# Summing both squared tiles of a pair on TensorE in the second and third pre-norm of a layer

## The reference, cut to what matters

```
def rmsnorm(x, g):
    xf = x.astype(F32)
    y = xf * lax.rsqrt(jnp.mean(xf * xf, axis=-1, keepdims=True) + RMS_EPS)
    return (y * g.astype(F32)).astype(x.dtype)
...
    h = rmsnorm(x, g[0]) * (1 + m[:, :, 0, 1]) + m[:, :, 0, 0]
    x = x + 0.5 * m[:, :, 0, 2] * rmsnorm(swiglu(h, wg[0], wu[0], wd[0]), g[1])
    h = rmsnorm(x, g[2]) * (1 + m[:, :, 1, 1]) + m[:, :, 1, 0]
    p = h @ w_in
...
    x = x + m[:, :, 1, 2] * rmsnorm(y, g[3])
    h = rmsnorm(x, g[4]) * (1 + m[:, :, 2, 1]) + m[:, :, 2, 0]
    x = x + 0.5 * m[:, :, 2, 2] * rmsnorm(swiglu(h, wg[1], wu[1], wd[1]), g[5])
```

## Time and profile before

| | |
|---|---|
| median of 3 runs | 1708.38 us (1708.3 to 1711.51) |
| span of the profiled execution | 1706.8 us (no other time is given for it) |
| PE, matmul | 1607.5 us busy, 94% of the span |
| VectorE (DVE) | 899.6 us busy, 53% |
| ScalarE (ACT) | 765.5 us busy, 45% |
| chain that ended last | PE 87%, DVE 6%, issue 3%, DMA 2%, ACT 2% |
| mean granted TensorE clock | 0.985 of full speed |

### The profile page before, as it was taken

How to read it: one execution, slowest core, us unless ns; L and a number is a source line. 1 busy time by engine, 2 the same in 40 slices (tenths; PEclk the granted TensorE clock), 3 DMA queues, 4 the chain that set the end, 5 groups by cost and what they waited for, 6 DMA issues and landing times.

```text
span 1706.8 us, 26956 instructions
## 1 busy us (share of the span) xinstructions
PE 1607.5 (94%) x9434; PEld 1462.8 (86%) x9434; DVE 899.6 (53%) x1597; ACT 765.5 (45%) x1176; POOL 17.8 (1%) x39
## 2 busy tenths in 40 slices
PE   6799999998988899999989999999898889999996
PEld 2399989996966699989979998999696669998996
DVE  5655544336685655544336554533667565554433
ACT  2355544325535555543255544432552555554332
POOL 0000000000000000000000000000000000000000
PEclk9999999999999999999999999999999999999998
DMA  6833685345501433474343368534550144337331
GB/s 232 333 107 125 249 294 182 130 159 182 181 1 38 173 123 123 137 282 138 129 167 100 124 247 293 191 124 165 181 181 1 36 163 130 124 126 298 132 124 65
DMA packets 70613, 268.20 MB, mean 157 GB/s; under 512 B 9387, under 2 KB 10444, under 8 KB 69900
## 3 DMA queue, kind: packets, MB, share of 16 engines
q1 hardware_dynamic: 67164, 248.96, 41.7%
q0 software_dynamic: 3376, 18.35, 2.8%
HBM read 260.73 MB, written 6.55 MB: 157 GB/s over the span
## 4 chain that ended last, share of the span: by engine, by line
PE 87%; DVE 6%; issue 3%; DMA 2%; ACT 2%; POOL 0%; DVEq 0%; SPq 0%; ACTq 0%; POOLq 0%
PE bank L529 26%; PE bank L531 25%; PE bank L530 25%; PE bank L538 4%; PE bank L867 1%; PE bank L829 1%; DVE y L1271 1%; DMA w_m<-w_mod 1%; DVE rstd L1266 1%; PE bank L753 1%; PE bank L617 1%; DMA f_cst<-tneg 1%; DVE sb_s L1457 1%; ACT prob_t L1068 1%; PE bank L856 1%
## 5 line engine op out<-in xcount | busy, mean ns | idle before, releaser
L1207 DVE TENSOR_TENSOR w_lo<-w_raw,w_hi 128x1024 fp32r<-128x1024 f32 (+2 forms) x288 | 373.6, 1297 | 527.5 <-ACT w_hi L927 526.6
L529 PE MATMUL bank<-h_hi,w_hi 128*128 128x386 f32 (+1 forms) x1760 | 606.3, 344 | 1.3 <-DVE w_lo L1207 0.8
L531 PE MATMUL bank<-h_hi,w_lo 128*128 128x386 f32 (+1 forms) x1760 | 596.1, 339 | 0.0
L530 PE MATMUL bank<-h_lo,w_hi 128*128 128x386 f32 (+1 forms) x1760 | 595.5, 338 | 0.0
L927 ACT ACTIVATE w_hi<-w_raw 128x1024 fp32r<-128x1024 f32 (+2 forms) x288 | 322.1, 1118 | 528.2 <-PE bank L531 527.6
L529 PEld LDWEIGHTS bank<-h_hi,w_hi 128*128 128x128 f32 x1760 | 332.0, 189 | 20.9 <-issue 14.0
L530 PEld LDWEIGHTS bank<-h_lo,w_hi 128*128 128x128 f32 x1760 | 332.8, 189 | 1.2
L531 PEld LDWEIGHTS bank<-h_hi,w_lo 128*128 128x128 f32 x1760 | 332.3, 189 | 0.0
L530 PE MATMUL bank<-hid_lo,w_hi 128*128 128x384 f32 x704 | 238.4, 339 | 0.0
L529 PE MATMUL bank<-hid_hi,w_hi 128*128 128x384 f32 x704 | 238.4, 339 | 0.0
L531 PE MATMUL bank<-hid_hi,w_lo 128*128 128x384 f32 x704 | 238.4, 339 | 0.0
(11 more groups left out here) (194 smaller groups left out, 1123.5 us busy)
## 6 DMA issues: line engine op xcount, KB each, us to landing
w_raw<-w_gu SPq DMA_DIRECT2D x176, 512.0 KB, 3.3
w_m<-w_mod SPq DMA_DIRECT2D x160, 512.0 KB, 6.3
w_raw<-w_dn SPq DMA_DIRECT2D x64, 704.0 KB, 4.0
w_raw<-w_in SPq DMA_DIRECT2D x26, 512.0 KB, 3.4
w_raw<-w_out SPq DMA_DIRECT2D x16, 512.0 KB, 3.4
cst<-consts POOLq DMA_DIRECT2D x8, 688.0 KB, 5.9
spec<-f_spec POOLq DMA_DIRECT2D x2, 2304.0 KB, 8.2
spc<-spec POOLq DMA_DIRECT2D x8, 576.0 KB, 5.1
```

Of the source, the lines that this page charges most:

```text
L529: mm(out, w_hi[:, wn, c], rhs_hi, start=first, stop=False)
L530: mm(out, w_hi[:, wn, c], rhs_lo, start=False, stop=False)
L531: return mm(out, w_lo[s][:, c], rhs_hi, start=False, stop=last)
L1207: TT(w_lo[unit % RAW][:, 0:n], w_raw[unit % RAW][:, 0:n], w_hi[:, unit % HIS, 0:n], ALU.subtract).then_inc(unit_lo.sem, 1)
```

## The change

VectorE's add of the two squared tiles goes, in the second and third pre-norm of each layer. PE waits for ScalarE's squares themselves and multiplies both squared tiles of a pair with the matrix of ones, two matmuls in place of one, all accumulated in the same bank; this is the code that the first pre-norm already used. ScalarE now waits for PE's reading of a buffer (xsq_used) before it squares into it again. The semaphore xsq_added goes.

```diff
                 for c in range(4):
-                    if n:
-                        pe.wait_ge(xsq_added.sem, xsq_added.at(layer, 4 * n + c - 3))
-                        last = mm(bank[STAT][:, 0:T], ones[:, :], sq[:, c % 2, :], start=c == 0, stop=c == 3)
-                    else:
-
-                        pe.wait_ge(xsq_done.sem, xsq_done.at(layer, c + 1))
-                        for k in range(2):
-                            last = mm(bank[STAT][:, 0:T], ones[:, :], xsq[:, c % 2, k, :], start=c == 0 and k == 0,
-                                      stop=c == 3 and k == 1)
+                    pe.wait_ge(xsq_done.sem, xsq_done.at(layer, 4 * n + c + 1))
+                    for k in range(2):
+                        last = mm(bank[STAT][:, 0:T], ones[:, :], xsq[:, c % 2, k, :], start=c == 0 and k == 0,
+                                  stop=c == 3 and k == 1)
                     last.then_inc(xsq_used.sem, 1)
...
-                    if n:
-                        act.wait_ge(xsq_added.sem, xsq_added.at(layer, 4 * n + c - 5))
-                    else:
-                        act.wait_ge(xsq_used.sem, xsq_used.at(layer, c - 1))
+                    act.wait_ge(xsq_used.sem, xsq_used.at(layer, 4 * n + c - 1))
                     A(xsq[:, c % 2, :, :], x[:, 2 * c:2 * c + 2, :], ACT.Square).then_inc(xsq_done.sem, 1)
...
-            dve.sem_inc(xsq_added.sem, 2)
...
-                if n:
-                    dve.wait_ge(xsq_done.sem, xsq_done.at(layer, 4 * n + c + 1))
-
-                    dve.wait_ge(xsq_used.sem, xsq_used.at(layer, 4 * n + c - 1))
-                    TT(sq[:, c % 2, :], xsq[:, c % 2, 0, :], xsq[:, c % 2, 1, :], ALU.add).then_inc(xsq_added.sem, 1)
                 for k in (2 * c, 2 * c + 1):
```

More of the change, by code:

```diff
@@ L339, in build @@
         x_new = S("x_new", 3 * 4, 4)
-        xsq_done, xsq_added, xsq_used = S("xsq_done", 12), S("xsq_added", 8, 2), S("xsq_used", 12, 2)
+        xsq_done, xsq_used = S("xsq_done", 12), S("xsq_used", 12, 2)
         pre_sd = S("pre_sd", 3)
```

## The result

The changed kernel takes 1714.93 us (median of 7 runs, 1713.57 to 1716.24) against 1708.38: 1.0037 of the time before, 95% interval 1.0026 to 1.0047, or 4.4 to 8.0 us more. It is slower by about 6.3 us where 4.3 were forecast, within the range given. The profiled execution took 1713.57 us itself, with a span of 1712.0 us, 5.2 us more than the profiled span of before.

The account below looks back on a forecast made before the run. The prediction took PE, busy in 94% of the span, to bound the kernel. Added matmuls 10.4 less earlier start 4.9 less waits 1.2 made +4.3 us onto 1708.38: 1712.7 us, range 1709.6 to 1716.4.

Parts of the forecast that it names:

- PE's added work: Four more statistics matmuls of 384 columns at each of four places, 16 times 0.65 us: 10.4 us lost.
- The earlier start: PE's first statistics matmul hangs on ScalarE's first square, not the add: 1.37 or 1.09 us a place, 4.9 us gained.
- The new wait: ScalarE's third and fourth squares wait for PE's reading of the buffer: costed at nothing, without cover up to 1.4 us a place.
- three signs of being wrong: PE waiting for the fourth square or a remainder; the clock at 1.00 through a place; places ending no later than before.
- the step on TensorE's clock: Low-clock stretches after PE's first statistics matmul, 3.1 to 5.6 us, stay as long, counted from the new start: no cost.
- The waits that go: PE's waits for VectorE between first and fourth statistics matmul, 0.11, 0.22, 0.59 and 0.27 us, vanish: 1.2 us gained.
- Rival 1: The clock rises at the same instants as before despite PE's earlier start: 2.5 us more lost, +6.8, 1715.2 us; chance 0.16.
- the forecast's assumption: At each place the low-clock stretch lasts as long as before, counted from PE's new start, costing nothing more.
- Rival 2: The clock rises early, after 3.1 us at each place: +2.4, 1710.8 us; chance 0.11.
- Rival 3: PE starts before the clock falls at all places, so low stretches go: -3.7, 1704.7 us, faster; chance 0.07.
- Rival 4: All the added work lands, as work starting earlier ends in another wait: +10.4, 1718.8 us; chance 0.04.

Follow-up runs that it names:

- the halves: The change in the second pre-norm of each layer alone, and in the third alone: 1709.89 and 1711.27 us against 1708.72 for the kernel before.
- rounded squares: Changed kernel with squares and ones in the rounded float type: 1704.23 us in all three pre-norms; 1702.89, later 1702.21, in second and third alone.
- the first pair: Kernel before with the change for the first pair of the second and third pre-norm alone, VectorE adding the other three: 1708.61 us against 1709.06.

## Why the prediction was right, and where it was not

*The direction and the terms.* PE's added work was right: 9.8 us between the changed kernel and the one without the second matmuls, for a forecast of 10.4, and 10.4 at equal low stretches. The earlier start was right as well: PE's idle time fell by 1.45 us in each place, 5.8 together for a forecast of 4.9, since ScalarE's first square in the second and fourth place also starts 0.36 us sooner after its update of x (4.86 us of waiting then, 4.50 now; the halves show 4.50 in places that they leave unchanged, too). The stretch from PE's first statistics matmul to the end of the fourth grew by 1.6, 2.9, 3.6 and 2.6 us, where 2 to 2.5 were forecast. The new wait costs nothing: ScalarE waits 1.25 to 2.61 us for PE ahead of its fourth square, VectorE 0.59 to 1.95 behind it, and PE for neither. None of the three signs of being wrong came.

*What failed* is the step on TensorE's clock: a low stretch of the same length "costs nothing more". That took the kernel before to pay half of each low microsecond already. It pays nothing in three of the four places: VectorE's chain of updates, adds and remainders sets 17.1 us there, and PE reaches that only when its low stretch exceeds about 4.5 us (17.67 us at 5.6; the 4.5 is an estimate from this one place, with half of each low microsecond lost). The chain of the third place, which left PE for VectorE ahead of the third pair, was the sign of it. By taking the adds out, the change lowered VectorE's floor, and by loading PE it put the place on PE's line, 16.1 us plus half the low stretch. So the right comparison is 17.1 against 16.1 + t/2 for a low stretch t: a gain only below 2 us, and none of the idle places seen had less than 3.1.

*The waits that go* were mis-sized for the same reason: the 1.2 us of them were read behind low stretches, which had held PE back and so covered VectorE. (The 0.11 us of the first place are no wait: its first product shows 0.55 us in place of 0.38, at the low clock.) At the full clock PE waits 1.53 us for one add in a single place. The two errors nearly cancel at the low stretches of the profile of before, and by that luck the sum came close: 1.1 us a place at 4.2 us in the runs with half of the change, or 4.4 in all, for a sum of 4.3. In the profiled execution low stretches of 4.7 us on average make that 4.8. What brings the runs to 6.3 is not shown place by place; the longer ones had the lower clock over the span, and above the floor a longer low stretch weighs on the changed kernel alone.

*The rivals.* Rival 1, that the clock rises at the instants at which it rose, gives a time close to the measured one. In the three changed kernels the 12 changed places have low stretches of 4.4 us on average, the eight unchanged ones of the kernel before and of the two halves 3.95; rival 1 would want the difference to be the 1.45 us of the earlier start. With single stretches from 3.1 to 6.3 us the time leaves the matter open between it and the forecast's assumption, but the windows speak for its mechanism. Added over the idle time and the 7.00 us behind it, the low level lasted 6.8 or 6.9 us in all four places of the kernel before and in three of the changed kernel, although PE started 1.45 us earlier in these: the stretches behind the start spread because the clock fell sooner or later in the idle time. In the changed kernel's first place the low level lasted 3.3 or 3.4 us in all in the two profiles, and there neither rival 1 nor the forecast's assumption holds. Rival 2 did not come: the low stretches were 3.4 to 6.3 us, and 2.4 us more lies below the interval. Rival 3's condition came about in the first place, where PE started ahead of the fall, but its consequence did not: the clock fell all the same. In the three other places it had fallen before PE's first matmul. Where PE was kept busy on purpose the low stretches went, for 7.3 to 8.4 us against rival 3's 8.0, and the change was indeed a gain. Rival 4's 10.4 us were not reached: the early start and the adds are worth 5 us. The Trainium skill's Perfetto Trace Analysis, in Optimization Strategy, says that the most contended engine can change from one stretch of a kernel to another; these places agree with it, PE being busy in 94% of the span and VectorE setting the end of these 17.1 us.

## What to carry to other kernels

A wait that the profile does not show was hidden here under a slow clock of the engine that would wait: before costing work moved from one engine to another, compare the lengths of the same place where the clock differs, because a length that did not move with it was set by the other engine here, as the run with a busy PE and its chain then showed. Work moved onto TensorE behind an idle time put these places on PE's line, low clock and all, so it wants to be short (rounded squares, 0.51 us a pair in place of 1.45) or to stand where PE is idle anyway (the first pair, by the lengths of the places alone: the runs do not tell its gain from none). An engine's share of the whole span, 94% here, did not say which engine set these four places.

## What the runs showed of the hardware that was not expected

22 otherwise useless matmuls, 5.2 us in PE's idle time, kept the granted clock at 1.00 through all four places in two kernels; without them it fell every time, with 5.19 or 6.64 us of idleness, in the changed kernel's first place only after PE had started again. The low stretch after PE's return varied from 3.1 to 6.3 us among places with the same work in front, since more or less of it had passed in the idle time; the runs of the changed kernel spread over some 5 us, the longer ones at the lower clock.
